# A chunked recurrence inside a long single-core kernel: state steps spread over the next pair, one product level in halves, one addition moved to GpSimd

## The reference, cut to what matters

```python
def rwkv7_step(S, inp):
    r_t, dec_t, k_t, v_t, kk_t, a_t = inp
    sa = jnp.einsum('bhij,bhj->bhi', S, -kk_t)
    S = (S * dec_t[:, :, None, :]
         + sa[..., None] * (kk_t * a_t)[:, :, None, :]
         + v_t[..., None] * k_t[:, :, None, :])
    y = jnp.einsum('bhij,bhj->bhi', S, r_t)
    return S, y
...
    _, y = lax.scan(rwkv7_step, S0, seq)
...
    bonus = (jnp.sum(rh * kh * r_k, axis=-1, keepdims=True) * vh).reshape(B, T, D)
```

## Time and profile before

| | us |
|---|---|
| median of 3 runs | 2526.11 |
| lowest and highest run | 2523.8, 2527.6 |
| the profiled execution | 2526.39 |
| its span, from the first to the last instruction | 2524.7 |
| TensorE busy in the span | 2405.5 (95%) |
| VectorE, ScalarE, GpSimd busy | 1129.9, 926.2, 1005.3 |
| the recurrence, from pair 0's first transposes to the last y copy | 167.7 |

### The profile page before, as it was taken

One profiled execution on the slowest core, in us unless ns is written; L12 is line 12 of the kernel. 1 busy time (PEld: TensorE's weight loads), 2 busy tenths in 40 slices (PEclk: granted clock), 3 DMA queues, 4 the chain that ended last, 5 costly groups with the idle time before them and its releaser, 6 DMA issues.

```text
span 2524.7 us, 34816 instructions
## 1 busy us (share of the span) xinstructions
PE 2405.5 (95%) x13680; PEld 1892.8 (75%) x13680; DVE 1129.9 (45%) x1852; ACT 926.2 (37%) x1542; POOL 1005.3 (40%) x584
## 2 busy tenths in 40 slices
PE   7999999999989888888999999999999999999998
PEld 5775667888866667775887888888667787888887
DVE  5113754203134567525433563362589333552462
ACT  3554653213236444324433322123333534322222
POOL 4341445444442222113553545345324444444344
PEclk9999899999999999989999999999999999999999
DMA  3212002223321110003321223222213221223222
GB/s 125 67 64 92 17 18 92 95 97 100 131 75 42 50 59 22 3 3 128 126 84 59 90 94 117 84 94 89 84 50 109 84 84 59 97 92 112 84 100 67
DMA packets 55588, 198.08 MB, mean 78 GB/s; under 512 B 6551, under 2 KB 8727, under 8 KB 54683
## 3 DMA queue, kind: packets, MB, share of 16 engines
q1 hardware_dynamic: 54509, 192.65, 22.5%
q10 hardware_dynamic: 941, 3.53, 0.4%
HBM read 194.06 MB, written 2.10 MB: 78 GB/s over the span
## 4 chain that ended last, share of the span: by engine, by line
PE 47%; DVE 6%; ACT 1%; issue 0%; DVEq 0%; ACTq 0%
PE ps L370 11%; PE ps L371 11%; PE ps L372 11%; DVE ps L2875 4%; PE ps L445 3%; PE ps L446 3%; PE ps L447 3%; PE ps L2718 1%; PE ps L2741 1%; PE ps L2888 1%; DVE ps L3037 0%; PE ps L2487 0%; PE ps L2728 0%; PE ps L2932 0%; PE ps L2518 0%; PE ps L2491 0%
## 5 line engine op out<-in xcount | busy, mean ns | idle before, releaser
L469 POOL TENSOR_TENSOR w_lo<-raw,w_hi 128x1024 fp32r<-128x1024 f32 x342 | 819.1, 2405 | 1008.1 <-ACT w_hi L461 1008.0
L370 PE MATMUL ps<-ahead_hi,w_hi 128*128 128x512 f32 x1216 | 481.6, 396 | 2.0 <-issue 2.0
L372 PE MATMUL ps<-ahead_hi,w_lo 128*128 128x512 f32 x1216 | 474.0, 390 | 0.0
L371 PE MATMUL ps<-ahead_lo,w_hi 128*128 128x512 f32 x1216 | 473.8, 390 | 0.0
L461 ACT ACTIVATE w_hi<-raw 128x1024 fp32r<-128x1024 f32 x342 | 352.9, 1049 | 169.4 <-PE ps L447 91.0
L370 PEld LDWEIGHTS ps<-ahead_hi,w_hi 128*128 128x128 f32 x1216 | 228.7, 188 | 53.3 <-issue 6.4
L371 PEld LDWEIGHTS ps<-ahead_lo,w_hi 128*128 128x128 f32 x1216 | 228.7, 188 | 50.7 <-issue 4.1
L372 PEld LDWEIGHTS ps<-ahead_hi,w_lo 128*128 128x128 f32 x1216 | 228.6, 188 | 48.0
L736 DVE TENSOR_TENSOR x_stream<-x_stream,ps 128x512 f32<-128x512 f32 x79 | 54.3, 687 | 468.0 <-PE ps L372 278.0
L3009 ACT ACTIVATE ffn_s<-ps 128x512 f32<-128x512 f32 x44 | 26.4, 599 | 322.2 <-DVE ps L3037 322.2
L445 PE MATMUL ps<-ffn_a_hi,w_hi 128*128 128x512 f32 x342 | 133.5, 390 | 3.0 <-DVE ffn_a_lo L3042 2.9
(11 more groups left out here) (415 smaller groups left out, 4395.1 us busy)
## 6 DMA issues: line engine op xcount, KB each, us to landing
raw<-in_wall SPq DMA_DIRECT2D x346, 512.0 KB, 3.3
x_stream<-in_x SPq DMA_DIRECT2D x8, 256.0 KB, 8.0
cw<-in_cmp_w SPq DMA_DIRECT2D x1, 2048.0 KB, 8.6
out_y<-x_stream SPq DMA_DIRECT2D x16, 128.0 KB, 1.9
lora_a<-in_lora_a ACTq DMA_DIRECT2D x1, 1152.0 KB
dist<-in_consts SPq DMA_DIRECT2D x1, 1088.0 KB, 11.7
lora_b<-in_lora_b ACTq DMA_DIRECT2D x1, 1024.0 KB
mem<-in_mem SPq DMA_DIRECT2D x1, 1024.0 KB, 4.9
```

Of the source, the lines that this page charges most:

```text
L370: pe.matmul(out, hi, src.hi[:, t, 0:width], start=first, stop=False)
L371: pe.matmul(out, hi, src.lo[:, t, 0:width], start=False, stop=False)
L372: return pe.matmul(out, lo, src.hi[:, t, 0:width], start=False, stop=last)
L469: e.tensor_tensor(self.w.lo[:, s, :], self.raw[:, s, :], as_float(self.w.hi[:, s, :]), ALU.subtract).then_inc(lo_r.sem, 1)
```

## The change

The state steps of the pair before are spread further over a pair. In TensorE's queue `u32_tensor` and `ak_v_tensor` now come in two halves of eight matmuls each, by chunk pairs. The first half of u32 waits for the first two of the four masks only and stands between state steps 4 and 5, the first half of ak_v between 5 and 6, the second halves behind 6, and y behind them. The spread of the bonus goes from bank 5 to bank 0 and from behind the seeds to behind y; the seeds stand behind `t32`. Since solved's second part writes bank 0, it waits for the bonus multiply (`bonus_out`).

In VectorE's queue the first masks stand behind S4 instead of S3, the second behind S5. The solve steps of batch 1 are divided anew: nine before and four behind the bonus multiply in pair 0, four and four in pairs 1 to 3 (what is left in pair 3).

Q is no longer made on VectorE. `output_scalar` copies its sums from banks 3 and 4 to SBUF in one ScalarE instruction behind both W, and `output_pool` adds R on GpSimd, in its queue behind the placement for the next pair. The first transposes of the next pair wait for the copy and both W; y waits for the add; the placement waits for the add of the pair before. On ScalarE the y copy goes behind the U and AX copies.

The diff, cut (left out: what only renames or repeats, and the new order in `tensor`, of which the rows above tell):

```diff
+        if p >= 2:
+            wait(g, "out_made", p - 1)
...
-            wait(pe, "moves_taken", 4 * p)
+            wait(pe, "moves_taken", 2 * p)
+            wait(pe, "out_kept", p)
         if first == 2 and p:
-            wait(pe, "bonus_out", p)
+            wait(pe, "ak_v_taken", p)
             wait(pe, "t32_taken", 2 * p)
...
+    def u32_tensor(self, pe, p, part):
         k, wait, done = self.k, self.wait, self.done
-        wait(pe, "placed", 6 * p + 6)
-        wait(pe, "zeroed", 3)
-        wait(pe, "masked", 4 * p + 4)
-        wait(pe, "by_token_taken", 4 * p + 4)
-        for q in range(8):
-            for e in range(2):
-                o = self.half(e)
-                mm = pe.matmul(k.ps[o, 6, 32 * q:32 * q + 32], self.PM[o, q, 128:192], self.Ta[o, q, :], start=True, stop=True)
-        done(mm, "u32")
-
-    def ak_v_tensor(self, pe, p):
+        if part == 0:
+            wait(pe, "placed", 6 * p + 6)
+            wait(pe, "zeroed", 3)
+            wait(pe, "by_token_taken", 4 * p + 4)
+        wait(pe, "masked", 4 * p + 2 * part + 2)
+        for hh in range(2):
+            for i in (2 * part, 2 * part + 1):
+                q = NB * hh + i
+                for e in range(2):
+                    o = self.half(e)
+                    mm = pe.matmul(k.ps[o, 6, 32 * q:32 * q + 32], self.PM[o, q, 128:192], self.Ta[o, q, :], start=True, stop=True)
+        if part:
+            done(mm, "u32")
+
+    def ak_v_tensor(self, pe, p, part):
         k, wait, done = self.k, self.wait, self.done
-        for q in range(8):
-            for e in range(2):
-                o = self.half(e)
-                mm = pe.matmul(k.ps[o, 5, 64 * q:64 * q + 64], self.PM[o, q, 256:320], self.VT[o, q % NB, self.half(q // NB)],
-                               start=True, stop=True)
-        done(mm, "ak_v")
+        for hh in range(2):
+            for i in (2 * part, 2 * part + 1):
+                q = NB * hh + i
+                for e in range(2):
+                    o = self.half(e)
+                    mm = pe.matmul(k.ps[o, 5, 64 * q:64 * q + 64], self.PM[o, q, 256:320], self.VT[o, i, self.half(hh)],
+                                   start=True, stop=True)
+        if part:
+            done(mm, "ak_v")
...
-        wait(pe, "t32_taken", 2 * p + 2)
-        wait(pe, "ak_v_taken", p + 1)
+        if part == 0:
+            wait(pe, "t32_taken", 2 * p + 2)
+            wait(pe, "ak_v_taken", p + 1)
+        else:
+            wait(pe, "bonus_out", p + 1)
...
+        if first == 1:
+            wait(pe, "out_made", p + 1)
...
-            done(v.tensor_tensor(self.Q[:, :, e, :], sums[:, :, 64:P], r, ALU.add), "moves_taken")
+
+    def output_scalar(self, act, p):
+
+        k, wait, done = self.k, self.wait, self.done
+        wait(act, "moves_taken", 2 * p + 2)
+        done(act.activation(self.Q[:, :, :, :].rearrange("p i e t -> p e i t"),
+                            k.ps[:, 3:5, :].rearrange("p e (i t) -> p e i t", i=NB)[:, :, :, 64:P], ACT.Copy), "out_kept")
+
+    def output_pool(self, g, p):
+
+        wait, done = self.wait, self.done
+        wait(g, "out_kept", p + 1)
+        wait(g, "placed", 6 * min(p + 2, KD))
+        q = self.Q[:, :, :, :].rearrange("p i e t -> p (i e t)")
+        done(g.tensor_tensor(q, q, self.RA[:, 0, p, :], ALU.add), "out_made")
 
     def u32_scalar(self, act, p):
...
         k, wait, done = self.k, self.wait, self.done
-        wait(pe, "ak_v_taken", p + 1)
+        wait(pe, "masked", 4 * p + 2)
         wait(pe, "bonus_kept", 1)
         wait(pe, "spread_loaded", 16)
-        done(pe.matmul(k.ps[:, 5, :], self.wide[0:WIDE, self.chunk(p)], self.bonus[0:WIDE, :], start=True, stop=True),
+        done(pe.matmul(k.ps[:, 0, :], self.wide[0:WIDE, self.chunk(p)], self.bonus[0:WIDE, :], start=True, stop=True),
...
         for p in range(KD + 1):
             if p < KD:
                 self.tokens_scalar(act, p)
+                self.u32_scalar(act, p)
+                self.ak_v_scalar(act, p)
             if p:
                 self.y_scalar(act, p - 1)
             if p < KD:
-                self.u32_scalar(act, p)
-                self.ak_v_scalar(act, p)
                 self.t32_scalar(act, p)
                 self.solved_scalar(act, p)
+                self.output_scalar(act, p)
...
-        for p in range(1, KD):
-            self.place(g, p)
+        for p in range(KD):
+            if p + 1 < KD:
+                self.place(g, p + 1)
+            self.output_pool(g, p)
...
-        def some(p, count):
-            for _ in range(count if p <= 3 else 0):
+        def some(p, first, later):
+            for _ in range((first, later, later, later, 0, 0, 0, 0)[p]):
                 next(steps, None)
-        for part in range(2):
-            self.masks_vector(v, 0, part)
         for p in range(KD + 1):
+            more, old = p < KD, p - 1
             if p:
-                for c in range(3):
-                    self.state_vector(v, p - 1, c)
-                if p < KD:
-                    self.masks_vector(v, p, 0)
-                self.state_vector(v, p - 1, 3)
-                if p < KD:
-                    self.masks_vector(v, p, 1)
-                for c in range(4, 7):
-                    self.state_vector(v, p - 1, c)
-            if p < KD:
-                some(p, 9)
+                self.state_vector(v, old, 0)
+                self.state_vector(v, old, 1)
+                self.state_vector(v, old, 2)
+                self.state_vector(v, old, 3)
+            if more:
+                self.masks_vector(v, p, 0)
+            if p:
+                self.state_vector(v, old, 4)
+            if more:
+                self.masks_vector(v, p, 1)
+            if p:
+                self.state_vector(v, old, 5)
+                self.state_vector(v, old, 6)
+            if more:
+                some(p, 9, 4)
                 self.bonus_vector(v, p)
+                some(p, 4, 4)
                 self.moves_vector(v, p)
```

65 lines of the change are left out of this document (36 added, 29 removed).

## The result

The changed kernel takes 2502.7 us, the median of four runs (2501.16 to 2505.64). Runs of the kernel before on the same chip have the median 2526.86 (2523.8 to 2529.24), so the ratio is 0.9908, with a 95% interval of 0.9895 to 0.9921: 24.2 us faster. The forecast was 2509.8. Now and then an execution of a kernel is over 1.5% longer as a whole, at a lower clock, and such ones are left out of the ratios. The profiled execution took 2501.16 us, 1.8 us more than its span.

The account below looks back on a forecast made before the run. Bound: the order of handoffs in the recurrence, and a clock that falls there. Pairs 1 to 7 gain 21.6 us, pair 0 loses 5.4, the end gains 0.4: 2526.4 less 16.6 is 2509.8 us, range 2503 to 2520.

Parts of the forecast that it names:

- The chain of handoffs: Steady pairs 4 to 7: the new order of handoffs starts the next pair at T+17.0 us instead of T+18.86.
- The clock: Pairs 1 to 7: the low clock after lone state steps costs 12.1 us; full clock mostly expected after the change.
- B: Rival: the clock still falls once in every pair, at the same cost as now; 2519.6 us, chance 0.20.
- D: Rival: TensorE never works densely enough to regain 2.4 GHz, so the kernel gets slower; 2549.5 us, chance 0.04.
- I take pair 1 to begin at 1.2 GHz for some 6 us: Start of pair 1: TensorE's idle time in pair 0 lowers the clock, costing 2.3 us.
- Each waits for one copy: Pair 0: about four VectorE instructions each wait for one GpSimd placement copy (0.62 to 0.66 us), +2.5 us; pair 1 +1.2.
- Rival C: Solve steps pass between the GpSimd copies unhindered; 2506.1 us, chance 0.13.
- Here a new wait bites: Pair 0: solved's second half waits for the bonus multiply until 998.8; with the later solve steps and copies, 5.4 us lost.
- hidden: Steady pairs: the GpSimd add of R ends before y wants it, with 5.3 us to spare, so costs nothing.
- no gain on the path: W to the next transposes stays 1.47 us: the added ScalarE copy takes the place of the removed Q adds.
- The end: Behind the last pair: the first state evict moves up by two adds (0.67 us) but waits for seeds; 0.4 us gained.
- the collision's bounds: Solve steps beside GpSimd copies: pair 0 from nothing to +3.7 us, pair 1 0 to 2.6; total 2507 to 2513 us.

Follow-up runs that it names:

- the kernel with the late steps: The changed kernel with the solve steps of pairs 1 to 3 divided two and six around the bonus multiply instead of four and four; one run, 2506.45 us.
- the kernel with 4 and 4 steps: The changed kernel with pair 0 doing four solve steps before the bonus multiply instead of nine, four behind as before; 2500.08 us, ratio 0.9889.

## Why the prediction was right, and where its sizes were off

**The chain of handoffs: right.** The steady pair was put at 17.0 us and takes 16.84; y was put at T+8.2 and starts at T+7.93, W at T+15.5 (T+15.31), the next transposes 1.47 behind W (1.53). The seven pairs at 0.16 us less each are 1.1 us. The experiments with the halves show the cause and not only the sum: put into the kernel before, they take 17.5 us off the seven; taken out of the changed one, they give 11.4 us back.

**The clock: right in kind.** The low clock was priced at 12.1 us in the seven; fillers in the kernel before give 10.9 back while costing about 1. After the change the clock is 1.00 in pairs 1 to 7, so B and D (0.24 together) didn't come.

**"I take pair 1 to begin at 1.2 GHz for some 6 us": wrong in place.** The clock did fall in pair 0 of the profiled run. But it fell at 997.64, in the wait for the bonus multiply, and had all but passed when pair 1 began: 0.50 from there to 1004.02, 0.99 in pair 1. The +2.3 is about nothing, and in four other profiles with the same steps in pair 0 the clock doesn't fall there at all. Inside pair 0 it costs nothing either, though solved's second half takes 1.76 us for 14 records where the first takes 1.1 for 16: W follows the last solve step without a gap (1001.73 + 0.70, W at 1002.45), so VectorE sets it, not TensorE. With the fall pair 0 is even 0.47 us shorter than without (19.31 and 19.78), since the copies then start later and meet fewer solve instructions.

**"Each waits for one copy": mis-sized.** The term was +2.5 in pair 0. Measured is 0.3 us an instruction, not 0.62 to 0.66: it waits for the rest of the copy in which it starts, not for a whole one. And two instructions met the copies in the profiled run, not four, for GpSimd began 2.12 us behind the start of the second half instead of 1.24, the low clock having stretched what it waited for. That makes 0.6 us; W came at 1002.45, not 1004.6, and near the lower bound of 1002.1 that the prediction gave. Where the clock didn't fall, the count was right: in the kernel with the late steps GpSimd begins 1.24 us behind the second half (999.37 and 998.13), four instructions of 0.70 to 0.72 us meet the copies in pair 0, and the term is 1.2. Pair 1 lost 0.57, not 1.2. Rival C, which took no hold-up at all, is not right either: the instructions do pay, half of what was reckoned.

The Trainium skill ("SBUF — State Buffer", "Who interferes with whom") calls the port pair that the two engines share an exclusive lock, held for the whole instruction by the one that issues first (this it says of VectorE's two-port modes), and counts a VectorE instruction with two SBUF inputs beside a GpSimd instruction that reads SBUF among those that contend. The traces agree, for the long subtraction of the earlier trace rows and for the short copies alike: the solve instruction ends 0.22 us behind the one and 0.26 behind the others. What went wrong was the step from there to a price. In the earlier trace rows the solve instruction started 0.15 us into an operation of 2.39, so it looked like a wait for the whole; beside copies of 0.7 us the 0.25 us by which it starts late count, and so does what it overlaps with the next copy.

**"Here a new wait bites": the wait came, but it is not what costs.** The second part of solved was put at 998.8 and ran at 998.59. W, however, hangs on VectorE, which has no idle time from 992.74 on: the four steps that were added behind the multiply, 4.0 us with the copies (998.45 to 1002.45), are what moves W from T+14.30 to T+17.75. The prediction's sum went this way too (998.7 to 1002.1 and the copies on top). The kernel with 4 and 4 steps shows that pair 0's loss is the division of the steps: there it takes 14.97 us, less than before the change (15.77).

**What was "hidden" is hidden.** Four more adds on GpSimd change no pair from 0 to 6 by more than 0.01 us; the 5.3 us to spare, forecast and found, were enough. (In the last chain less is to spare: there y waits 1.06 us for them.) Of the move of Q the prediction said "no gain on the path"; the reverse is 0.17 us faster in the seven, so this too stands.

**The end and the rest.** From W to the last y copy 0.9 us were gained, not 0.4. But the clock there was 0.88 after and 0.72 before; with the same end at 0.71 the kernel with 4 and 4 steps gains 0.3, so the 0.4 was about right and the rest is luck. Another 2.1 us lie behind the recurrence, where nothing was changed and TensorE's busy time is 2.0 us less (1342.99 and 1340.96). That is luck too, as far as the profiles tell: with the code there unchanged this part takes 1369.9 to 1372.1 us in the 14 of them, and before the change it was at the low clock for 23.8 us, after it for 18.4.

**The sum.** Forecast -16.6, measured -25.3 between the spans: 2.3 for the clock in pair 1, 1.1 for the steady pair, 0.6 for pair 1, 1.9 for pair 0, 0.5 for the end and 2.3 outside the recurrence make 8.7. Of these some 2.8 (the end and outside) are no effect of the change. The median lies 0.3 us below the stated lower bound of 2503: the range leaned on the collision's bounds, all of which were losses, and left no room on the side of gain for the clock's place or for what varies outside.

## What to carry to other kernels

When short matmuls wait for each other through a second engine, look for work that can be cut in halves and laid between them: it fills the gap and keeps the clock up, and the two effects were of like size here. Fillers, matmuls that compute nothing, tell in one run how much of a slow stretch is the clock. Of what is strewn into an early pair count each instruction that stands ahead of the handoff, and look whether its engine has idle time left there: in pair 0 VectorE had none, and each added step went into the pair's length, while TensorE's new wait of 3 us lay beside it and, by the trace, cost nothing. And the price for two engines that exclude each other is the rest of the operation that is under way, not a whole one.

## What the runs showed of the hardware that was not expected

- **VectorE beside short GpSimd copies.** A VectorE add or multiply between SBUF tiles takes 0.70 to 0.73 us instead of 0.41 beside a row of 32-partition copies of 0.60 to 0.64 us, and the copies grow by 0.06 to 0.1 each. It ends 0.26 to 0.28 us behind the copy in which it started, just as it ends 0.22 behind an operation of 2.39 us. Shorter ones of 0.27 to 0.34 us take 0.61 to 0.76, so they pay more, up to 0.46. One that is under way when the copy starts pays nothing, and neither do the adds of W beside the copies, one input of which lies in PSUM (0.41 to 0.43 us each).
- **GpSimd in a row.** A 128x512 add takes 1.26 to 1.28 us alone, but four in a row 4.03 us and eight 8.02, 1.0 each. The price from single rows was too high for a series.
- **The clock between runs.** The same instructions ran at 1.00 in one profile and at 0.95 in another between 270 and 400 us, and the start of pair 0 lies up to 6.9 us apart in the profiles.
